# The two products of a feed-forward stage computed by Strassen's method, seven block products in place of eight

## The reference

```python
        x = x + jnp.concatenate([attn, y], axis=-1) @ w_out[l]
        h2 = rms_norm_2(x, norm2_w[l])
        up = causal_dwconv(h2 @ w_up[l], conv_ffn_w[l], conv_ffn_b[l])
        g, val = jnp.split(up, 2, axis=-1)
        x = x + (jax.nn.gelu(g) * val) @ w_down[l]
    return x
```

## Time and profile before

| what | us |
|---|---|
| median of 3 runs | 3683.96 (3677.12 to 3684.14) |
| profiled execution: span from the first to the last instruction | 3686.7 |
| last stretch of the span, from the first feed-forward matmul (2896.0) to its end | 790.7 |
| PE busy in the whole span | 3296.3 (89%) |
| DVE busy in the whole span | 1805.7 (49%) |

### The profile page before, as it was taken

How to read it: one execution, slowest core, us unless ns; L and a number is a source line. 1 busy time by engine, 2 the same in 40 slices (tenths; PEclk the granted TensorE clock), 3 DMA queues, 4 the chain that set the end, 5 groups by cost and what they waited for, 6 DMA issues and landing times. The chain is left out here.

```text
span 3686.7 us, 62343 instructions
## 1 busy us (share of the span) xinstructions
PE 3296.3 (89%) x27450; PEld 2755.4 (75%) x27450; DVE 1805.7 (49%) x2463; ACT 1178.6 (32%) x1648; POOL 393.9 (11%) x272
## 2 busy tenths in 40 slices
PE   5599999798986689897999989998777999999999
PEld 3488888688886479855899977776546788888887
DVE  6454455455653542253555534753443463636364
ACT  0444334222222322255444422542552211111111
POOL 0122221000000112110000012211102000000000
PEclk9799999778876899999999999999788999999999
DMA  8112231422212321324112013122002111111112
GB/s 346 43 70 101 105 125 72 122 72 72 72 43 94 131 92 46 117 85 173 57 59 63 31 61 126 47 78 94 29 18 86 52 40 57 42 56 43 54 45 76
DMA packets 145995, 294.53 MB, mean 80 GB/s; under 512 B 10048, under 2 KB 86976, under 8 KB 140224
## 3 DMA queue, kind: packets, MB, share of 16 engines
q1 hardware_dynamic: 126608, 212.95, 17.1%
q0 software_dynamic: 19120, 77.60, 6.2%
HBM read 211.22 MB, written 79.30 MB: 79 GB/s over the span
## 5 line engine op out<-in xcount | busy, mean ns | idle before, releaser
L60 PE MATMUL ev_ps<-h_hi,ev_w_hi 128*128 128x512 f32 (+1 forms) x792 | 288.5, 364 | 36.5 <-POOL ev_w_lo L360 35.2
L60 PE MATMUL ff_ps<-h_hi,ff_w_hi 128*128 128x512 f32 x768 | 300.1, 391 | 2.2 <-DVE ff_w_lo L3043 2.2
L61 PE MATMUL ff_ps<-h_lo,ff_w_hi 128*128 128x512 f32 x768 | 299.8, 390 | 0.0
L62 PE MATMUL ff_ps<-h_hi,ff_w_lo 128*128 128x512 f32 x768 | 299.7, 390 | 0.0
L62 PE MATMUL ev_ps<-h_hi,ev_w_lo 128*128 128x512 f32 (+1 forms) x792 | 281.1, 355 | 0.0
L61 PE MATMUL ev_ps<-h_lo,ev_w_hi 128*128 128x512 f32 (+1 forms) x792 | 281.1, 355 | 0.0
L3043 DVE TENSOR_TENSOR ff_w_lo<-ff_w,ff_w_hi 128x1024 fp32r<-128x1024 f32 (+1 forms) x80 | 89.5, 1119 | 339.5 <-ACT ff_w_hi L3018 339.5
L60 PEld LDWEIGHTS ev_ps<-h_hi,ev_w_hi 128*128 128x128 f32 x792 | 150.5, 190 | 75.1 <-POOL ev_w_lo L360 36.0
L3018 ACT ACTIVATE ff_w_hi<-ff_w 128x1024 fp32r<-128x1024 f32 (+1 forms) x80 | 78.0, 975 | 326.3 <-PE ff_ps L62 324.0
L60 PEld LDWEIGHTS ff_ps<-h_hi,ff_w_hi 128*128 128x128 f32 x768 | 144.8, 189 | 34.0 <-DVE ff_w_lo L3043 3.8
L62 PEld LDWEIGHTS ff_ps<-h_hi,ff_w_lo 128*128 128x128 f32 x768 | 144.8, 189 | 30.3
(11 more groups left out here) (501 smaller groups left out, 8065.7 us busy)
## 6 DMA issues: line engine op xcount, KB each, us to landing
ff_w<-in_w_up SPq DMA_DIRECT2D x48, 512.0 KB, 3.5
ev_w<-in_ev_w_in POOLq DMA_DIRECT2D x33, 512.0 KB, 3.9
ada_wt<-in_ada_w POOLq DMA_DIRECT2D x12, 1024.0 KB, 8.5
ada_wt<-in_ada_w SPq DMA_DIRECT2D x12, 1024.0 KB, 8.7
...
sc_ar<-ar SPq DMA_DIRECT2D x20, 512.0 KB, 6.1
```

The lines of the kernel that those rows point to most:

```text
L60: nc.tensor.matmul(out, w_hi, x_hi, start=start, stop=False)
L61: nc.tensor.matmul(out, w_hi, x_lo, start=False, stop=False)
L62: return nc.tensor.matmul(out, w_lo, x_hi, start=False, stop=stop)
```

## The change

**The up product.** Gate tile t and value tile t + 24 are taken together as unit u = t (24 units). The 1024 x 256 weights and the 1024 x 1024 activations are split into 2 x 2 blocks, and a unit is seven block products of 12 matmuls each: 84 in place of 96. The sums of activation blocks T1 to T4 are formed once, the ones for B11, B21, B22 split in `phase_second_out`, the four T at the start of `phase_ffn`. The sums of weight blocks are formed per unit: four DVE additions (`add`). The products run in the order P1, P5, P6, P2, P7, P3, P4; ACT copies P1, P5 and the partial sum U2 out of PSUM (`keep`), matmuls then go on adding to the same bank, and DVE adds the kept parts (`corner`). The taps' first product moves from DVE to ACT (`tap`).

**Where things lie.** x after `phase_second_out` goes to DRAM (`g.x3`) and comes back as one 4 MB load behind the last unit. The gated rows go to DRAM (`g.mid`), one 512 KB store per unit by POOL, and come back in pairs.

**The down product.** It runs behind all units as 7 products i = 0 to 6 (P1, P2, P6, P5, P7, P3, P4) of 12 steps k each: step s = 12 i + k, 84 steps of 12 matmuls. A step needs one moving operand (512 tokens) and one weight operand, both split by ACT (`down_hi`) and DVE (`down_t_lo`, `down_w_lo`) into one of three pairs of slots. For i = 2, 3 and 5 DVE also forms weight sums from raw weights in a ring of four 512 KB buffers, one step ahead (`down_combos(s + 1)`), in i = 3 an operand sum as well, in i = 1 two shared operand sums per step (`down_shared`). One DMA brings the weights of two steps, as pieces of 1 KB. DVE adds a finished product to x in two instructions at k = 2 and 3 of the next product (`evacuate`).

The diff, cut to what is spoken of:

```diff
+                    nc.scalar.activation(h[:, m], x[:, m % 2], ACT.Copy, scale=scale(m)).then_inc(h_done, 1)
+                    if m < HK:
+                        nc.scalar.activation(b11[:, 0, m], x[:, m % 2, first], ACT.Copy, scale=scale(m)).then_inc(hi_done, 1)
+                    else:
+                        nc.scalar.activation(b21[:, 0, m - HK], x[:, m % 2, first], ACT.Copy, scale=scale(m)).then_inc(hi_done, 1)
+                        nc.scalar.activation(b22[:, 0, m - HK], x[:, m % 2, second], ACT.Copy, scale=scale(m)).then_inc(hi_done, 1)
                     if m:
                         act.wait_ge(summed, m)
-                    nc.scalar.activation(sq[:], x[:, m], ACT.Square).then_inc(squared, 1)
+                    nc.scalar.activation(sq[:], x[:, m % 2], ACT.Square).then_inc(squared, 1)
...
                 for m in range(KD):
...
+                    dve.wait_ge(h_done, m + 1)
+                    j = m - HK
+                    if m < HK:
+                        low(b11, m, h[:, m, first], hi_count(m) + 1)
+                        dve.wait_ge(lo_done, hi_count(m) + 1)
+                        nc.vector.tensor_tensor(h[:, m, first], h[:, m, second], h[:, m, first], ALU.subtract).then_inc(t1_done, 1)
+                    else:
+                        low(b21, j, h[:, m, first], hi_count(m) + 1)
+                        low(b22, j, h[:, m, second], hi_count(m) + 2)
+                        dve.wait_ge(t1_done, j + 1)
+                        nc.vector.tensor_tensor(h[:, j, second], h[:, m, second], h[:, j, second], ALU.subtract).then_inc(t3_done, 1)
+                        dve.wait_ge(lo_done, hi_count(m) + 2)
+                        dve.wait_ge(t3_done, j + 1)
+                        nc.vector.tensor_tensor(h[:, m, second], h[:, m, second], h[:, j, first], ALU.subtract).then_inc(t2_done, 1)
+                        dve.wait_ge(t2_done, j + 1)
+                        nc.vector.tensor_tensor(h[:, m, first], h[:, m, first], h[:, m, second], ALU.subtract).then_inc(t4_done, 1)
...
     nc = g.nc
-    PARTS = FFN_TILES // FFN_PART
-    UP, DOWN = 2 * FFN_PART, KD
-    PER = UP + DOWN
-    N = PARTS * PER
-    SLOTS = 4
...
+        p1, p5, u2 = h[:, 0, first], h[:, 0, second], h[:, 1, first]
+        rows = [h[:, 2], h[:, 3]]
...
+        of_pair = lambda a, k: a.rearrange("p (m k c) -> p m k c", m=HK, k=2)[:, :, k % 2]
...
+        RING_STEP = [12 + 2 * j + 1 for j in range(NP_)] + [12 * i + 2 * j + 1 for i in (2, 3, 5) for j in range(NP_) for x in range(2)] + [72 + 2 * j + 1 for j in range(NP_)]
...
+        t_slot, w_slot = (lambda s: 2 * (s % 3)), (lambda s: 2 * (s % 3) + 1)
...
+                def down_weights(half, ks, j):
+                    part, pair_ = divmod(ks * NP_ + j, FFN_PART // 2)
+                    return g.ins["w_down"][part, HK * half:HK * half + HK, :, 2 * pair_:2 * pair_ + 2].rearrange("m p k c -> p m (k c)")
...
+                def load_ring(q):
+                    name, j = ring_use[q]
+                    if q < 4:
+                        sp.wait_ge(w_lo_done, PROD * (NU - 1) if q < 2 else PROD * NU)
+                    else:
+                        sp.wait_ge(dw_lo, RING_STEP[q - 4] + 1)
+                    sp.dma_start(ring(q), down_weights(0 if name == "a12" else 1, 1, j) if name != "a21" else down_weights(1, 0, j)).then_inc(loaded[q % 4], 16)
+
+                for j in range(NP_):
+                    load_mid("b11", j)
+                    load_mid("a11", j)
+                for j in range(NP_):
+                    load_mid("b21", j)
+                    load_ring(j)
+                    load_mid("b22", j)
+                    load_mid("b12", j)
+                for q in range(NP_, len(ring_use)):
+                    load_ring(q)
...
+                for u in range(NU):
+                    pool.wait_ge(prod, u + 1)
+                    pool.dma_start(g.mid[u], acc[u % 2][1]).then_inc(mid_stored[u % 2], 16)
+                for j in range(2):
+                    pool.wait_ge(mid_stored[j], 16 * (NU // 2))
+                pool.dma_start(x[:], g.x3).then_inc(x_in, 16)
...
+                def up(u, j):
+                    pe.wait_ge(w_lo_done, PROD * u + j + 1)
+                    if u == 0 and MOVES[j] >= T1:
+                        pe.wait_ge(t_lo_done, MOVES[j] - T1 + 1)
...
+                        pe.wait_ge(p1_kept, u + 1)
+                    if j == P7:
+                        pe.wait_ge(u2_kept, u + 1)
+                    if j == P3:
...
+                def down(s):
+                    i, k = divmod(s, NK)
+                    pe.wait_ge(dt_lo, s + 1)
+                    pe.wait_ge(dw_lo, s + 1)
...
+                def keep(dst, u, j, name, free, kept):
+                    act.wait_ge(done, PROD * u + j + 1)
+                    if u:
+                        act.wait_ge(free, u)
+                    else:
+                        act.wait_ge(t_lo_done, 3 if dst is p5 else 1)
+                    A(dst, bank(u, name), ACT.Copy).then_inc(kept, 1)
+
...
+                for u in range(NU):
+                    more = u + 1 < NU
+                    if u:
+                        corner(u - 1)
+                    hi(u, 6)
+                    if u:
+                        tap(u - 1, 0)
+                        tap(u - 1, 1)
+                    keep(p1, u, P1, "Y", c11, p1_kept)
+                    if more:
...
+                def corner(u, name, j, kept, mine, x_, half):
+                    dve.wait_ge(done, PROD * u + j + 1)
+                    dve.wait_ge(kept, u + 1)
+                    if u:
+                        dve.wait_ge(conv, 4 * u)
+                    else:
+                        dve.wait_ge(t_lo_done, 3)
+                    tt(rows[x_][:, half], bank(u, name), {"X": p1, "Y": p5, "Z": u2}[name], ALU.add).then_inc(mine, 1)
+
...
+                def down_combos(s):
+                    i, k = divmod(s, NK)
+                    if i in (2, 3, 5):
+                        qa, qb = ring_no(i, k, 0), ring_no(i, k, 1)
+                        a, b = of_pair(ring(qa), k), of_pair(ring(qb), k)
+                        for q in (qa, qb):
+                            dve.wait_ge(loaded[q % 4], ring_count(q))
+                        kept = of_pair(pairs["a11"][k // 2], k)
+                    if i == 2:
+                        tt(kept, kept, a, ALU.subtract).then_inc(w_comb, 1)
+                        dve.wait_ge(w_comb, 2 * k + 1)
+                        tt(b, b, kept, ALU.subtract).then_inc(w_comb, 1)
+                    if i == 3:
+                        tt(a, a, b, ALU.add).then_inc(w_comb, 1)
+                        if k >= 2:
+                            dve.wait_ge(dt_lo, s - 1)
+                        dve.wait_ge(t_comb, 24 + k)
+                        tt(spare[:, k % 2], mid("b22", k), mid("b11", k), ALU.subtract).then_inc(t_comb, 1)
+                    if i == 5:
+                        tt(a, a, b, ALU.subtract).then_inc(w_comb, 1)
+                        dve.wait_ge(w_comb, 36 + 2 * k + 1)
+                        tt(a, a, kept, ALU.add).then_inc(w_comb, 1)
+                    if i == 6:
+                        tt(mid("b21", k), mid("b21", k), mid("b11", k), ALU.subtract).then_inc(t_comb, 1)
+
...
+                def evacuate(i, b):
+                    if i == 0:
+                        dve.wait_ge(x_in, 16)
+                    dve.wait_ge(steps, NK * (i + 1))
+                    if i in (1, 4, 5):
+                        dve.wait_ge(evac, 2 * {1: 0, 4: 3, 5: 2}[i] + 2)
+                    q = QUAD[INTO[i]][:, 2 * b:2 * b + 2]
+                    tt(q, group(i)[:, 2 * b:2 * b + 2], q, ALU.add).then_inc(evac, 1)
...
+                for s in range(3, NS):
+                    if s + 1 < NS:
+                        down_combos(s + 1)
+                    down_t_lo(s)
+                    down_w_lo(s)
+                    i, k = divmod(s, NK)
+                    if i == 1:
+                        down_shared(k)
+                    if i and k in (2, 3):
+                        evacuate(i - 1, k - 2)
+                    if s in (3, 4):
+                        scale_rows(L, s - 3)
+                    if 5 <= s < 9:
+                        convolve(L, (s - 5) // 2, 1 + (s - 5) % 2)
+                    if s == 9:
+                        multiply(L)
+                for m in range(HK):
+                    dve.wait_ge(last, m + 1)
+                    q = x[:, HK + m, first]
+                    tt(q, ps[:, m], q, ALU.add).then_inc(evac, 1)
 
```

More of the change, by code:

```diff
@@ new lines, in phase_ffn @@
+    loaded = [g.sem(f"ff_loaded{j}") for j in range(4)]
+    combos, w_hi_done, w_lo_done, t_hi_done, t_lo_done = (g.sem(f"ff_{x}") for x in ("combos", "w_hi", "w_lo", "t_hi", "t_lo"))
+    sums, logs, rs_ready, done = (g.sem(f"ff_{x}") for x in ("sums", "logs", "rs", "done"))
+    p1_kept, p5_kept, u2_kept, c21, c11, c22, c12 = (g.sem(f"ff_{x}") for x in ("p1", "p5", "u2", "c21", "c11", "c22", "c12"))
```

(10 more changed lines are left out.)

531 lines of the change are left out of this document (372 added, 159 removed).

## The result

The changed kernel takes **3643.76 us** (median of four, 3639.7 to 3657.36); the kernel before, run beside it, 3684.05 us. The ratio is 0.9897, 95% interval 0.9875 to 0.992. So the change gains 40.3 us where 50.6 were forecast; 3633.5 was 10.3 us too low, and the time lies inside both the stated range and the likeliest case's own.

What follows compares the result with a forecast made beforehand. The prediction took PE, busy with matmuls throughout the feed-forward stage, as the bound. Its terms, -97.9 + 8.3 + 4.5 + 33 + 2 - 0.5 = -50.6 us, gave 3633.5 us, range 3598 to 3668.

Steps and rivals of the forecast that it cites:

- the likeliest case: Whole kernel: the sum as worked out holds, with its own range of 3620 to 3650 us; chance 0.58.
- matmuls: Feed-forward stage: 3024 matmuls in place of 3456, 432 fewer at 0.2265 us each, -97.9 us.
- start: Start of feed-forward: P1 begins 0.5 us later, PE stands 6.8 before P6 for ACT's copy, low clock 1.0; +8.3 us.
- x: Early down product: the 4 MB load of x lands late, DVE waits in step 14 and PE starves; +4.5 us.
- ring: Down product, i = 2, 3, 5: DVE's sums wait for late weight loads, a pair of steps takes 8.05 us; +33 us.
- clock behind the waits: Down product and start: PE's idling brings low-clock stretches, mostly hidden in its waiting, costing at the edges; +2 us.
- end: End of the kernel: four 512-wide additions, three of them under PE's last matmuls; -0.5 us.
- DVE in the up part: Up product: DVE needs 16.9 us of PE's 19.0 per unit, margins of 1.4 and 1.7 us; cost 0.
- DVE becomes the bound of the up part: Rival, up product: extra waiting per DVE instruction lengthens each unit; 3652 to 3675 us, chance 0.15.
- loads in time: Rival, down product: ring loads land in under 4 us, so they cost nothing; 3598 up to 3612 us, chance 0.13.
- a pair of loads takes 9 us: Rival, down product: 14 pairs lose 3.6 us more each, 50 us, whole gain gone; slower for any reason: chance 0.08.
- the whole down-projection at 1.2 GHz: Rival, down product: PE stays at the low clock, 10.3 us per pair of steps, +30 us; 3664 us, chance 0.06.

Runs made afterwards that it cites:

- d2: Changed kernel with two more DVE instructions in each up-projection unit from the third on; stage (last output matmul to end of span) 759.3 us.
- d4: Changed kernel with four more DVE instructions in each up-projection unit from the third on; a unit takes 20.16 us for 19.03.
- d6: Changed kernel with six more DVE instructions in each up-projection unit from the third on; a unit takes 21.6 us for 19.04.
- e3: Changed kernel with ACT's copy of the first unit's P1 moved right behind the conversion of T2; stage 752.3 us for 761.1, median 2.5 us lower.
- e1: Changed kernel with DVE's weight sums for the next down-projection step placed behind the current step's two low parts; 3608.1 us, stage 728.7 us.
- h1: Changed kernel with only half of each ring load brought from the second product's end on (wrong result); 25.3 us less than the changed kernel run again.
- c1: Changed kernel with ring loads taken from up-projection weights in 4 KB pieces (wrong result); 8.1 us less than the changed kernel run again.
- e2: Changed kernel with DVE's addition of P1's result to x moved to down-projection steps 20 and 21 from 14 and 15; 3632.8 us.

## Why the prediction was nearly right, point by point

All in the stage. Before: 11.55 us up to the first feed-forward matmul, 3456 x 0.2265 = 782.8, 3.4 for the low clock behind the start, and 4.5 from the last matmul to the end, together 802.3. After: P1's first matmul comes 11.18 us behind the last output matmul, the up part ends at 478.7 (456.6 of it matmuls), the down-projection 278.2 later (228.3 of it matmuls), and 4.3 remain.

```
term                       predicted   measured
matmuls                    -97.9       -97.9
start                       +8.3        +7.1
ACT's GELU (steps 5 to 7)    -          +1.2
x                           +4.5        +7.8
ring                       +33         +33.2
clock behind the waits      +2          +7.6
end                         -0.5        -0.2
sum                        -50.6       -41.2
```

- **Matmuls, DVE in the up part**: right. Behind the first, PE stood in no unit, at 0 cost: each lasts 19.04 us. DVE is busy for 16.7 us of a unit, 16.9 forecast, and d2, d4 and d6 measured a margin of 1.76 beside the 1.4 and 1.7 read from the order. The rival in which DVE becomes the bound of the up part is refuted by one row (453.31 of 453.31). What the prediction quotes for that rival from the Trainium skill (VectorE: DVE Perf Modes, The DRAIN you can't avoid) is only half of it: the section goes on that a next operation that isn't held starts earlier. So the overlapping starts don't disagree with it.
- **The start**: right in mechanism and nearly in size: 6.8 forecast, 7.24 measured, and ACT's copy it was (e3). The 11.55 us of the earlier trace rows up to the first matmul are 11.18 now, where 0.5 more was forecast.
- **The ring**: right in mechanism (e1), in form (h1) and in size; the size is partly luck. L = 5.4 was picked between 4.8 and 6.5, ends that give 25 to 48 us, by setting 1 KB pieces between two prices. c1 puts the pieces at some 0.35 us where 0.6 was allowed for, and 4 KB pieces at 5.1 where 4.8 was read; the two errors nearly cancel. Steps 27 to 45 started 23.0 us later than at PE's pace, a gap of 2.9 opened the series and the last four gaps, in P3, are 7.3. The rival "loads in time" is refuted by L = 5.4, the one in which a pair of loads takes 9 us too. The Trainium skill (DMA: Bandwidth & Descriptors, Anatomy of one DMA), quoted in the prediction, gives its fit for DMAs that GpSimd issues, and the prediction set it on loads that SyncE issues; by that estimate the ring would have cost 19.
- **x comes back late: the first term that was mis-sized.** Steps 0 to 15 should take 15 x 2.72 = 40.8 us and took 49.8. Of these 9.0 us, 1.2 were lost at steps 5 to 7, behind ACT's GELU, which the prediction put at nothing and which no edit here takes away; 7.8 is the wait for x, for 4.5. Three steps of the sum fell short. The multiplication on DVE ends 45.0 us behind the start of the last unit, not 41.4. Some 1.65 us of this are the same GELU, which holds up ACT's split and with it DVE's; the rest is the work of steps 5 to 9, convolutions included, which DVE takes without a further pause:

```profile
3389.93 1.06 ACT L3212 ACTIVATE h<-h 128x1024 f32<-128x1024 f32 x1 [3.39 <-DVE h L3341]
3390.90 0.61 ACT L3231 ACTIVATE ff_w_hi<-ff_mem 128x512 fp32r<-128x512 f32 x1
...
3391.54 0.69 DVE L3384 TENSOR_TENSOR ff_w_lo<-ff_mem,ff_w_hi 128x512 fp32r<-128x512 f32 x1 [1.65 <-ACT ff_w_hi L3231]
...
3397.55 1.22 DVE L3347 TENSOR_TENSOR h<-h 128x1024 f32<-128x1024 f32 x1
```

  "The store takes 0.6 + 3": from the end of the multiplication to the load's issue it is 6.9, the store alone 6.03 (2.6 was the price of a lone store), in a stretch where the DMA engines are busy for 0.99 of the time at 351 GB/s. The load took 14.4 for 12.7. So x landed 66.3 us behind the start of the last unit instead of 58 to 62. By the prediction's own rule that would cost 10.3; but only one of the two additions stands ahead of step 15's splits, not both, which gives back 1.2: 9.1, and 9.0 were measured. The store takes 5.9 to 6.2 us in the other runs too, the load 12.9 to 14.6, and the wait, where it is kept, 6.1 to 8.0. That the loads beside them stretch both transfers is argued from the DMA share; no run varies it. e2 took away 13.0 us where the wait (7.8) and the low clock behind it (2.7: steps 15 to 23 last 27.2 us for 24.5, clock 0.84 in the row 3405.50:3438.00) come to 10.5; the rest is within the 5 us by which this part varies.
- **The clock: the second.** "In the ring a low-clock stretch hides in PE's own waiting" is right inside a series of late pairs:

```profile
3477.40:3485.60 8.20, 5.72 (x24) 4.42 (x25) 5.08 (x9) 2.41 (x4) 0.00 (x0) 1.00 0.41 130
3485.60:3493.48 7.88, 7.31 (x24) 5.56 (x25) 5.00 (x9) 1.78 (x3) 0.00 (x0) 0.78 0.43 133
```

  Both pairs last 8 us, at a clock of 1.00 and of 0.78. But "at its edges, +2" was too little: 3.1 us between the wait for x and the first late pair, and 4.5 behind the last ones of P5 and among those of P3, 7.6 in all. The rival with the whole down-projection at 1.2 GHz did not come: the granted clock over all of it, 3372.85 to 3651, is 0.95.

The two mis-sized terms, 3.3 for x and 5.6 for the clock, with the 1.2 that was left out and 0.5 at the ring and the end, less 1.2 at the start, are the 9.4 us between the sums.
